# Unit lengths of four heads from one root and one reciprocal, spread by a product, with all key products ahead of the transposes

## What is computed

```python
qkv = silu(short_conv(concat([qa, ka, va]), conv_w))      # 5 taps, per channel; 12 groups of 128 channels
q, k, v = split(qkv)                                      # 4 heads of 128 channels each
q = l2_norm(q) * DK_A ** -0.5                             # x * rsqrt(sum(x * x) + EPS), per token and head
k = l2_norm(k)
# chunks of 64 tokens: products k k^T and q k^T of each chunk, then a triangular solve and a scan
```

## Time and profile before

| | |
|---|---|
| median of 3 runs | 2172.15 us (2171.51 to 2176.67) |
| the profiled execution, its own time | 2179.57 us |
| its span, first to last instruction | 2178.1 us |
| TensorE matmuls busy | 1841.9 us (85%) |
| VectorE busy | 668.1 us (31%) |
| ScalarE busy | 489.0 us (22%) |
| chain that ended last, by engine | PE 65%, DMA 11%, DVE 7%, issue 6% |

### The profile page before, as it was taken

How to read it: one execution, slowest core, us unless ns; L and a number is a source line. 1 busy time by engine, 2 the same in 40 slices (tenths; PEclk the granted TensorE clock), 3 DMA queues, 4 the chain that set the end, 5 groups by cost and what they waited for, 6 DMA issues and landing times.

```text
span 2178.1 us, 31197 instructions
## 1 busy us (share of the span) xinstructions
PE 1841.9 (85%) x12295; PEld 1106.5 (51%) x12295; DVE 668.1 (31%) x1310; ACT 489.0 (22%) x1116; POOL 153.5 (7%) x186
## 2 busy tenths in 40 slices
PE   3988999998989877888579799899889897788885
PEld 2658764556645452232255586555675455323223
DVE  1494342314111241221218743423131112312113
ACT  3372431112200121111136425111130002011111
POOL 2004110100000000000100320110000000000000
PEclk8899999997899969999879999999869997899997
DMA  9224412331030518999842531140500334199990
GB/s 334 93 78 158 157 54 78 44 137 42 1 116 4 205 63 311 395 393 395 297 155 78 194 118 66 68 83 2 177 1 1 116 116 154 67 395 393 394 369 29
DMA packets 165603, 344.66 MB, mean 158 GB/s; under 512 B 21098, under 2 KB 23234, under 8 KB 165344
## 3 DMA queue, kind: packets, MB, share of 16 engines
q1 hardware_dynamic: 162528, 338.44, 43.2%
q0 software_dynamic: 2944, 4.39, 1.0%
HBM read 339.39 MB, written 3.41 MB: 157 GB/s over the span
## 4 chain that ended last, share of the span: by engine, by line
PE 65%; DMA 11%; DVE 7%; issue 6%; PEld 4%; ACT 4%; DVEq 2%; SPq 1%; PEldq 1%; ACTq 0%; POOL 0%; POOLq 0%
PE PS L747 19%; DMA arena<-in_w_expert_up_dram 9%; PE PS L1425 8%; PE PS L754 6%; PE PS L1333 4%; PE PS L1450 3%; PE PS L719 2%; PEld PS L747 2%; PE PS L1183 2%; PE PS L1311 2%; PE PS L795 1%; PE PS L901 1%; PE PS L909 1%; PE PS L1291 1%; PE PS L1394 1%
## 5 line engine op out<-in xcount | busy, mean ns | idle before, releaser
L747 PE MATMUL PS<-hT,ring 128*128 128x384 f32 x1568 | 538.1, 499 | 23.4 <-DMA ring<-in_w_in_dram 17.4
L747 PEld LDWEIGHTS PS<-hT,ring 128*128 128x128 f32 x1568 | 303.6, 195 | 240.4 <-issue 45.3
L1425 PE MATMUL PS<-ring,arena 128*48 128x512 f32 x768 | 234.1, 608 | 33.8 <-DMA arena<-in_w_expert_up_dram 18.0
L1479 ACT ACTIVATE arena<-PS 128x512 f32<-128x512 f32 (+3 forms) x246 | 114.9, 497 | 502.0 <-PE PS L719 180.6
L1425 PEld LDWEIGHTS PS<-ring,arena 128*48 128x48 f32 x768 | 70.2, 125 | 192.1 <-issue 166.0
L754 PE MATMUL PS<-ring,hT 128*128 128x256 f32 (+1 forms) x384 | 132.0, 501 | 11.6 <-DVE arena L2069 11.2
L719 PE MATMUL PS<-const,arena 128*128 128x128 f32 (+2 forms) x413 | 66.4, 310 | 70.9 <-DVE arena L2300 34.9
L1425 PE MATMUL PS<-arena 128*48 128x512 f32 x256 | 119.4, 622 | 0.0
L754 PEld LDWEIGHTS PS<-ring,hT 128*128 128x128 f32 x384 | 74.4, 197 | 62.3 <-issue 44.0
L719 PEld LDWEIGHTS PS<-const,arena 128*128 128x128 f32 (+2 forms) x413 | 53.1, 167 | 102.5 <-issue 69.1
L2300 DVE TENSOR_TENSOR arena<-arena,PS 48x512 f32<-48x512 f32 x32 | 22.1, 690 | 243.9 <-ACT arena L1759 243.9
(11 more groups left out here) (328 smaller groups left out, 2293.4 us busy)
## 6 DMA issues: line engine op xcount, KB each, us to landing
ring<-in_w_expert_gate_dram SPq DMA_DIRECT2D x32, 2048.0 KB, 16.6
ring<-in_w_in_dram SPq DMA_DIRECT2D x26, 2048.0 KB, 9.7
ring<-in_ada_w_dram SPq DMA_DIRECT2D x24, 2048.0 KB, 16.5
ring<-in_w_expert_up_dram SPq DMA_DIRECT2D x16, 2048.0 KB, 20.8
ring<-in_w_expert_down_dram SPq DMA_DIRECT2D x16, 2048.0 KB, 18.8
arena<-in_w_expert_up_dram SPq DMA_DIRECT2D x16, 2048.0 KB, 21.8
arena<-in_w_expert_down_dram SPq DMA_DIRECT2D x16, 2048.0 KB, 19.0
ring<-in_w_out_dram SPq DMA_DIRECT2D x4, 2048.0 KB, 13.6
```

The lines of the kernel that those rows point to most:

```text
L747: ins = mm(out, w[:, k, 128 * c:128 * c + 128], hT[:, k, :], start=k == 0, stop=k == KT - 1)
L1425: ins = mm(PS[64 * n:64 * n + ROWS, u % 2, :], xs_e[:, u % 2, k, :], expert_view(3 * u + n)[:, k, :], start=k == 0, stop=k == KT - 1)
L1479: return f(out, in_, ACT.Copy)
```

## The change

The sum of squares of a head goes into 32 rows of PSUM only, and four heads share a bank: heads 0 to 3 in bank 5, heads 4 to 7 in bank 4. One root and one reciprocal then serve four heads. A product with a new table `lead` (one row of 32 is ones, the others zero) spreads each head's 32 rows to all 128 rows of a bank, and the unit product reads that bank. On TensorE the squared length of head i moves up to stand behind group i + 2, the first of them straight behind the gate products; the spreading products stand behind groups 7, 8 and 10. `delta_rows` moves behind the wait for the last unit product, and all three `delta_kk` come ahead of the three `delta_tok`, with a wait for the pad of group 11 in place of that for its silu. The table makes the constants 128 columns wider.

```diff
+LENGTHS_AFTER = {7: (0, 1, 2), 8: (3,), 10: (4, 5, 6, 7)}
+LENGTH_BANK = (6, 7, 5, 6, 7, 6, 5, 4)
...
+    tabs["lead"] = np.broadcast_to(r % 32 == 0, (128, 128))
...
-                    mm(PS[:, 4 + j % 4, 0:N], ones, sq_in[:, j % 2, :], start=True, stop=True).then_inc(T["conv_pe"].mark(("ss", j)), 1)
...
+                    mm(PS[32 * q:32 * q + 32, 5 - i // 4, 0:N], ones[:, 0:32], sq_in[:, i % 2, :], start=True, stop=True)\
+                        .then_inc(T["conv_pe"].mark(("ss", i)), 1)
...
+                def length_of(i):
+
+                    if i % 4 == 0:
+                        pe.wait_ge(done["conv_dve"], at("conv_dve", l, ("inv", i // 4)))
+                    if i == 3:
+                        pe.wait_ge(done["conv_dve"], at("conv_dve", l, ("unit", 0)))
+                    if i == 4:
+                        pe.wait_ge(done["conv_dve"], at("conv_dve", l, ("unit", 3)))
+                    own = slice(32 * (i % 4), 32 * (i % 4) + 32)
+                    pe.sem_inc(apart["pe"], 1)
+                    mm(PS[:, LENGTH_BANK[i], 0:N], K("lead")[own, :], nrm[own, i // 4, :], start=True, stop=True)\
+                        .then_inc(T["conv_pe"].mark(("bc", i)), 1)
...
+                for j in range(12):
                     blk = conv_channels(blk, j)
...
+                    if j == 2:
+                        pe.wait_ge(done["gate_dve"], at("gate_dve", l, "lf"))
...
                     if j == 4:
                         pe.wait_ge(done["gate_dve"], at("gate_dve", l, "done"))
-                    if j >= 4:
-                        squared_length(j - 4)
+                    if 2 <= j < 10:
+                        squared_length(j - 2)
+                    for i in LENGTHS_AFTER.get(j, ()):
+                        length_of(i)
...
+                pe.wait_ge(done["conv_act"], at("conv_act", l, ("pad", 10)))
+                pe.wait_ge(done["conv_dve"], at("conv_dve", l, ("unit", 7)))
                 for t in TO:
                     delta_rows(t)
-                pe.wait_ge(done["conv_dve"], at("conv_dve", l, ("unit", 7)))
+                pe.wait_ge(done["conv_act"], at("conv_act", l, ("pad", 11)))
+                for t in TO:
+                    delta_kk(t)
                 pe.wait_ge(done["conv_act"], at("conv_act", l, ("silu", 11)))
                 for n in range(TILES):
-                    delta_kk(TO[n])
                     delta_tok(n)
...
-                    if 3 <= j < 11:
-                        i = j - 3
+                    if 0 < j <= 8:
+                        i = j - 1
...
+                    if j in (5, 9):
+                        n = j // 5 - (j == 5)
+                        act.wait_ge(done["conv_pe"], at("conv_pe", l, ("ss", 4 * n + 3)))
+
+                        s = 1.0 if n else 128.0
+                        f(nrm[:, n, 0:N], PS[:, 5 - n, 0:N], ACT.Sqrt, bias=EPS * s, scale=s)\
+                            .then_inc(T["conv_act"].mark(("root", n)), 1)
...
+                    if j in (5, 9):
+                        n = j // 5 - (j == 5)
+                        v.wait_ge(done["conv_act"], at("conv_act", l, ("root", n)))
+                        V.reciprocal(nrm[:, n, 0:N], nrm[:, n, 0:N]).then_inc(T["conv_dve"].mark(("inv", n)), 1)
+                    for i in LENGTHS_AFTER.get(j, ()):
+                        v.wait_ge(done["conv_pe"], at("conv_pe", l, ("bc", i)))
+                        TT(qkvT[:, i, :], qkvT[:, i, :], PS[:, LENGTH_BANK[i], 0:N], ALU.mult).then_inc(T["conv_dve"].mark(("unit", i)), 1)
```

More of the change, by code:

```diff
@@ L393, in build_step @@
             "gate_pe": ["proj", "cum"], "gate_act": ["exp", "ln", "ecum"], "gate_dve": ["biased", "lf", "args", "done"],
-            "conv_pe": [s for j in rng(12) for s in [("p", j)] + [("ss", j - 4)] * (j >= 4)],
+            "conv_pe": [s for j in rng(12) for s in [("p", j)] + [("ss", j - 2)] * (2 <= j < 10)
+                        + [("bc", i) for i in LENGTHS_AFTER.get(j, ())]],
             "conv_act": [s for j in rng(13) for s in [("pad", j)] * (j < 12) + [("silu", j - 1)] * (j > 0)
-                         + [("sq", j - 3)] * (3 <= j < 11) + [("root", j - 4)] * (4 <= j < 12)],
-            "conv_dve": [s for j in rng(12) for s in [("conv", j)] + [("unit", j - 4)] * (j >= 4)],
-            "delta_pe": [("row", t) for t in TO] + [s for t in TO for s in (("kk", t), ("tok", t))] + [("xt", t) for t in TO]
+                         + [("sq", j - 1)] * (0 < j <= 8) + [("root", j // 5 - (j == 5))] * (j in (5, 9))],
+            "conv_dve": [s for j in rng(12) for s in [("conv", j)] + [("inv", j // 5 - (j == 5))] * (j in (5, 9))
+                         + [("unit", i) for i in LENGTHS_AFTER.get(j, ())]],
+            "delta_pe": [("row", t) for t in TO] + [("kk", t) for t in TO] + [("tok", t) for t in TO] + [("xt", t) for t in TO]
             + [s for i in rng(5) for s in [("p", i, t) for t in TO] + [("q", i, t) for t in TO]]
@@ L828, in conv_channels @@
                     return blk + (j % 4 == 3)
-                def squared_length(j):
-                    pe.wait_ge(done["conv_act"], at("conv_act", l, ("sq", j)))
-                    if j >= 4:
-                        pe.wait_ge(done["conv_act"], at("conv_act", l, ("root", j - 4)))
-                    mm(PS[:, 4 + j % 4, 0:N], ones, sq_in[:, j % 2, :], start=True, stop=True).then_inc(T["conv_pe"].mark(("ss", j)), 1)
-                for j in range(3):
-                    blk = conv_channels(blk, j)
@@ L840, in _ @@
[L840 to L846, removed]
@@ L847, in _, with squared_length @@
-                ins.then_inc(T["gate_pe"].mark("cum"), 1)
-                for j in range(3, 12):
-                    blk = conv_channels(blk, j)
+                def squared_length(i):
+                    pe.wait_ge(done["conv_act"], at("conv_act", l, ("sq", i)))
+                    q = i % 4
+                    mm(PS[32 * q:32 * q + 32, 5 - i // 4, 0:N], ones[:, 0:32], sq_in[:, i % 2, :], start=True, stop=True)\
[11 more added lines that the diff above has]
+                        .then_inc(T["conv_pe"].mark(("bc", i)), 1)
@@ new lines, in _ @@
+                for j in range(12):
+                    blk = conv_channels(blk, j)
+                    if j == 2:
+                        pe.wait_ge(done["gate_dve"], at("gate_dve", l, "lf"))
+                        for t in range(TILES):
+                            for d in range(2):
+                                mm(PS[:, 6, 16 * t + 8 * d:16 * t + 8 * d + 8], K(f"tri{d}"), g_lf[:, t, d, :], start=True, stop=True)
+                        gl = g_lf.rearrange("p t d h -> p (t d h)")
+                        for n, m in enumerate(("block", "half0", "half1")):
+                            ins = mm(PS[:, 6, 48 + 48 * n:96 + 48 * n], K(m), gl, start=True, stop=True)
+                        ins.then_inc(T["gate_pe"].mark("cum"), 1)
```

## The result

The changed kernel takes 2189.56 us (median of 13 runs, 2183.13 to 2197.78); the kernel before took 2176.67 in the same comparison (13 runs), 4.5 more than the median that the forecast started from. The ratio is 1.0059, interval 1.004 to 1.0078: 12.8 us slower, 8.7 to 17. The direction was forecast; the time lies 2.06 us above the range. The profiled execution took 2191.27 us, its span 2189.9. In the changed kernel p is L752, ss L839, bc L852, the rows L881, the keys L887, the transposes L724, the adaLN blocks L800.

What follows compares the result with a forecast made beforehand. VectorE's bound was to give way to the matmul queue. Idle, restart, products and shape changes, against old times, gave 4.45 us a layer; 2 x 4.45 + 0.2 = 9.1 us on 2172.15 made 2181.3, range 2174 to 2187.5.

Steps and rivals of the forecast that it cites:

- The wait: Behind the gate products, the first squared length waits for ScalarE's square until 92.99; the matmul queue idles 7.83 us.
- The restart: Low clock behind the new idle, at the first squared length and next channel products: 2.4 us, between 1.95 and 2.9.
- The products: Matmul queue from first squared length to last channel products: nine channel groups 46.44 us, eight squared lengths 5.20.
- The entries: Changes of product shape between channel groups, squared lengths and spreading products: 17 a layer at 0.18 us, 3.06.
- The eight bc: Spreading products in groups of three, one and four, partly overlapping on different rows: 3.55 us, bounds 1.95 to 5.20.
- bc(4): Spreading product of head 4: VectorE's second reciprocal not in the way, the queue having 6.2 us of its own work.
- p(11): Last group of channel products in the stage: done at 154.64 us, against 142.37 before.
- Keys and blocks: Behind the channel products: three key groups take 2.83 us, warm; adaLN blocks start at 167.3, 4.45 us later.
- Even: Shape changes free, each spreading group takes the time of one: -0.2 us per layer, 2172.0; chance 0.27 (within 6.5 us).
- Faster: Narrow products run beside the projections, so squared lengths, spreading and shape changes vanish: -7.4 us per layer, 2157.6; chance 0.06.
- Slower still: One more 2.7 us matmul-queue stop a layer, among small products behind the stage: 2186.7 us; chance above +15 us 0.07.
- Sum: 2 x 4.45 + 0.2 = 9.1 us: Whole program: two layers' stages each 4.45 us longer, 0.2 for loading the wider constant table.

Runs made afterwards that it cites:

- The wait alone: Kernel before with only ScalarE's squares and the squared lengths two groups earlier, the first straight behind the gate products: 2186.03 us against 2174.71, 1.0058.
- the change without it: Changed kernel with only the first four squared lengths moved, two behind the fifth channel-product group and two behind the sixth: 2166.33 us against 2174.71, 0.996.
- full-width ss: Changed kernel with squared lengths as products of the full array, 128 x 128 weights, four heads accumulated in one bank: 2186.89 us, 1.0063.
- the table alone: Kernel before with only the table of 128 more constant columns, which nothing reads: 2176.3 us, 1.0001.
- before with forty: Kernel before with 40 empty instructions a layer in TensorE's queue, where it waits for the last unit product: 2176.45 us against 2175.65, 0.9997.
- third execution: The changed kernel, unaltered, measured and profiled a third time against the kernel before: 2190.97 us against 2178.82, 1.0054.

## Why the prediction was right and wrong

**The wait.** ss(0) was put at 92.99 after 7.83 us of idle; it came at 93.51 after 7.85, in a layer that began 0.52 later. The wait alone, put into the kernel before, made its stages 12.0 us longer, and the change without it has stages 15.4 us shorter than before. So the direction was right for the forecast's reason.

**The restart.** 2.4 was taken; 2.34 in layer 1, 1.61 in layer 2 (1.49 + 6.24 less 6.12).

**The products.** The entries were 17 x 0.18; the chain shows 0.20 at each p and 0.11 at an ss behind a p (0.76 for 0.65). The Trainium skill's rule (TensorEngine Tiling (Array Packing), Key Properties), that a change of the tiling mode drains the engine, agrees with these prices: with full-width ss they vanish at ss (0.65 and 5.16) and stay beside bc (5.36). What the trace shows is the price alone, not a drain. The eight bc were 3.55 and three entries of 0.18, 4.09; they took 0.85 + 0.84 + 1.33 = 3.02. Four in line would be 2.60, so 1.33 with the entry is 1.95 times as fast. The 3.07 that the Trainium skill gives for four products on 32 rows each (TensorE: Matmul & The Clock Gate, Measured speedup vs the span model) is not reached here. This term was too high by 1.1. A stall of 0.5 ahead of bc(4), where VectorE's second reciprocal ends last, was not in the sum: the forecast set 6.2 against 6.2 there and left out what lies between pad, convolution and reciprocal. p(11) was to end at 154.64 and ended at 148.94 + 5.36 = 154.30, 0.86 early if the later start of the layer is taken off.

**Keys and blocks.** 2.83 for the keys, 2.77 measured, at clock 1.00; adaLN at 167.3, measured 167.07. Less the later start of the layer, the stage is 3.70 longer, and 3.21 in layer 2, where 4.45 was summed.

**The rivals.** Even needed free changes of shape and groups of bc in the time of one: three bc did take it (0.85 against 0.84), four did not, and the changes were not free. Faster needed narrow products beside p; ss stands between two p as before. Slower still named a new 2.7 us stop; none came, the old ones moved.

**The step that failed** is the last line of the sum, "Sum: 2 x 4.45 + 0.2 = 9.1 us", with the median of 2172.15 under it. The 0.2, put there for the wider table alone, stood for everything outside the two stages, and nothing was allowed for the clock elsewhere: it measured 5.9 in the first comparison (12.8 - 6.9), 9.7 and 4.8 in the two others, about 1 less against the mean stage of four profiles. The stages gave 6.9 where 8.9 was summed, so the difference of 12.8 is 3.7 over the 9.1: 5.7 too little outside, 2.0 too much inside, which cancel in part by luck. And the kernel before came out at 2176.67, 4.5 above the median of three runs that I built on. The 3.7 and the 4.5 together carry the time past the range; neither would alone.

**What the rest is.** Over the 14 profiles of the table the time outside the stages goes with the low clock outside the stages: correlation 0.96, 0.35 us for each us of low clock. The kernel after has 368 to 378 us of it, the two profiles of the kernel before 351 and 334. The timed executions say the same, since span and mean granted clock of 204 of them are on record; I take off the stage and its low clock as the profiles have them, for the kernel before the mean of the four. Outside the stages the 88 executions of the kernel before then have on average 345 us at the low clock, the 32 of the kernel after 361; the other six kernels built on the change have 357 to 371, the wait alone, the table alone and before with forty 338 to 346. The time outside is 2020 us before and 2027 after, and at 0.34 us for each us of low clock, the slope over all 204, some 5 of these 7 us go with the clock. That the clock makes this time is argued from the correlation and not shown. The largest spread is in the products of attention in each layer, in which the clock falls in every kernel; the same products took 56.9, 63.9 and 65.1 us in layer 1 of three profiles of the kernel after, 57.8 and 62.9 in two of the kernel before. Busy time by stretch, the kernel after first, then its third execution:

```profile
522.90:579.80 56.90, 51.12 (x249) 42.30 (x248) 19.62 (x35) 21.01 (x53) 0.00 (x0) 0.71 0.00 1
```

```profile
526.00:591.10 65.10, 59.42 (x248) 49.82 (x248) 19.61 (x35) 21.22 (x53) 0.00 (x0) 0.61 0.00 1
```

The same 248 or 249 products, at clock 0.71 and 0.61: 8.2 us apart in one kernel. One pair of profiles therefore says little about the rest.

**What stays open** is why kernels with shared lengths meet more of it. In the runs all seven such kernels lie 5 to 12 us above what their stage gives, by their ratio; of those with eight roots, the wait alone lies 0.6 above, the table alone 2.2 above, and before with forty 0.3 below. The table, the order of the keys, the place of the squares and the fall near 190 us are not it, as far as the intervals tell (4 to 6 us either way); the place of the queue's stops costs time in the profiles, but moved by forty instructions it changed nothing in the runs. Not tried: giving VectorE and ScalarE their old load back, and the spreading products by themselves.

## What to carry to other kernels

When a wait leaves an engine's queue, look at what the new order puts at the head of it: one product asked for 7.85 us early cost 19.6 us of idle and restart in two layers, more than the 15.4 that the stages won without it, and put behind the two product groups that had filled the gap it made a loss of 0.6% a gain of 0.4%. A stage's sum can be right within about a microsecond a layer and the whole still miss by the granted clock elsewhere; several profiles of the kernel before show how far that moves by itself. And a base of three runs was off by 4.5 us, half of the forecast effect.

## What the runs showed that was not expected

- The matmul queue's stops belong to places in the instruction stream: 40 empty instructions moved them by 18 to 20 products, in two kernels. Their length varies: behind the 35th W product it was anything from nothing to 1.25 us.
- Two narrow ss on different columns take 0.90 us together, three bc on different rows 0.85, one alone 0.76 to 0.84.
- The clock after 3.2 us of idle fell in six of eight layers of four profiles; after 7.8 us it fell each time.
